# Query, key and weight preparation in the attention projections and the linear attention scan of a two-layer hybrid block

## Chip, core and metric

The kernel runs on one core of one Trainium2 chip. The metric is the device time of one execution in microseconds (us). The engines are named as in the profile: PE is TensorE's matmul (PEld its weight load), DVE is VectorE, ACT is ScalarE, POOL is GpSimd and SP is SyncE, which starts the transfers.

## What is computed

Two layers of one block over 256 context tokens and 1024 latent tokens of width 1024. In each layer one input projection feeds four groups of heads, which are gated, concatenated and projected out:

```python
for l in range(DEPTH):
    hx = rmsnorm(x, norm_g[l]) * (1.0 + sc[:, None]) + sh[:, None]
    px = split_cols(hx @ w_in[l])
    a_l, a_c = diff_attention(px[0:3], ...)
    b_l, b_c = mlstm_mixer(px[3:8], ...)
    c_l, c_c = gla_mixer(px[8:12], ...)
    d_l, d_c = window_gqa(px[12:15], ...)
    y = jnp.concatenate([a_l, b_l, c_l, d_l], axis=-1) * jax.nn.silu(px[15])
    x = x + gt[:, None] * (y @ w_out[l])
```

Three pieces matter here. Both attentions (A: differential, 16 groups of 32 for q and k; D: windowed, 6 groups of 64) normalise q and k and turn them by an angle of the token's place:

```python
q = rmsnorm(q, qn_g)                       # per group of 32 or 64 columns
def _rotate(xh, ang):
    x1, x2 = jnp.split(xh, 2, axis=-1)
    return jnp.concatenate([x1 * cos - x2 * sin, x1 * sin + x2 * cos], axis=-1)
```

The gated linear attention (C, `gla_mixer`) is a scan with a state of 128 x 256 and a decay for each channel:

```python
inter = jnp.einsum('bhtd,bhdv->bhtv', q * jnp.exp(bc), smat)
a = jnp.einsum('bhtd,bhtsd,bhsd->bhts', q, jnp.exp(rel), k)
smat = jnp.exp(b_end)[..., None] * smat + ...
```

## The kernel before

The program is one sequence of stages, each with an instruction list written out by hand for every engine and semaphores between them; an all-engine barrier ends each stage. Nothing is reordered by a scheduler: what stands first in an engine's list runs first. In each of the two layers the order is modulation, norm, B (mLSTM), C (projection, then scan), A, D, gates, output.

**Projections.** `SplitProduct` multiplies in 32-bit parts: every operand is a high part (a rounded copy) and a low part (the rest), and three products are summed. Step i handles one 128-row slice k of one group g of the plan. ACT's `high` copies the tokens' high part (L420, 128x640); DVE's `low` casts the weights' high part and subtracts for their low part (`split_weights`, L383 and L384), then subtracts the tokens' low part (L437); PE's `multiply` (L456) then runs the 15 matmuls of a step. Three buffers (`BUFS` = 3) let ACT and DVE run ahead.

**project_qk** is called for A (L1696; four groups of 8 steps: q and k of tokens 0 to 639, the same of 640 to 1279, then v of each half with weights of 256 columns) and for D (L1903; two groups, v in the same slab). The ten token tiles t of 128 are worked on between the steps, those of a half (`HN` = 5) in the next group's steps: ACT's `keep` squares a tile (L1462), copies it from PSUM to `raw` (L1467) and, for D, v (L1466). DVE's `reduce`, `means`, `refine` and `norm` (L1530 to L1544) make and apply the reciprocal root, in between ACT's `roots` (L1478, L1479, a table load each). POOL multiplies by the gain (L1515) and by the cosine into `rot` (L1520). DVE's `rotate` multiplies by the sine with the two quarters of a pair exchanged, in four instructions (L1555), and adds (L1563 in A; L1569 in D). In D, PE transposes each turned tile (`turns`, L1436: tiles 0 and 1 after step 14, the others after step 15) and ACT keeps it (L1453). `rot` has two slots: POOL's cosine product of tile t waits, for t >= 2, until tile t-2 was turned by DVE (A) or transposed by PE (D). D's second half has no steps beside it: its norm and rotation stand after step 15.

**C's scan** visits 20 tiles, forward and backward in turn. ACT takes the exponentials of a visit (L1241, 8 x 128 columns), POOL scales k (L1229, L1231), DVE scales q (`scale_q`: L1338 a copy of one column, L1339 5 x 128 columns, L1341 128 columns) one visit ahead, PE multiplies (`levels`, `fresh`, `exponents` two visits ahead, `out` one behind), DVE picks the maps out of PSUM (L1370, three per visit) and `finish` updates the state two visits behind (L1347 and L1351 or L1353). `levels` of a visit waits for the three picks of the visit before; `finish` waits for `out`.

## Time and profile before

| | |
|---|---|
| time, median of 3 runs | 2638.15 us (2637.92 to 2640.21) |
| the profiled execution: its time | 2636.37 us |
| its span, first to last instruction | 2634.6 us |
| PE busy | 2109.6 us, 80% |
| DVE busy | 1827.8 us, 69% |
| ACT busy | 1117.2 us, 42% |
| POOL busy | 413.4 us, 16% |
| C's scan, layer 0 and 1 | about 392 to 500 and 1738 to 1850 us |
| A's projection | about 517 to 642 and 1864 to 1989 us |
| D's projection | about 909 to 1009 and 2233 to 2334 us |

Busy shares are averages over stages with different limits, so each stage is read by itself: which engine sits idle, and what ends its idle time. The execution's time has 1.8 us around its span, and lies 1.8 us under the median. The granted clock of PE is a share of its full rate: 1.00 is 2.4 GHz, 0.50 is 1.2 GHz.

### The profile page before, as it was taken

Reading aid. Unit: us, or ns where it says so; the run is one execution under the profiler, and the core shown is the slowest. Engines: PE = TensorE matmul, PEld = TensorE weight load, DVE = VectorE, ACT = ScalarE, POOL = GpSimd, SP = SyncE. Lnnn points to the kernel's source line nnn. Section 1 sums busy time; section 2 is a strip of 40 time slices with the busy share of each in tenths; the row PEclk is TensorE's granted clock in tenths of the full one; section 3 lists DMA queues with packets and bytes.
Section 4 is the critical chain, followed back from the end, with each engine's and each line's share of the span. In section 5 each row is a group of like instructions: output and inputs, shape, how many; then the busy total and the mean of one; then the engine's idle time right before and its main releaser. Section 6 shows DMA issues by size and latency. Waiting matters only on the chain. (4 is left out here: it accounts for less than half of the span.)

```text
span 2634.6 us, 38349 instructions
## 1 busy us (share of the span) xinstructions
PE 2109.6 (80%) x14612; PEld 1765.6 (67%) x14612; DVE 1827.8 (69%) x3505; ACT 1117.2 (42%) x2156; POOL 413.4 (16%) x414
## 2 busy tenths in 40 slices
PE   4968779786888776899987778979767877858988
PEld 2757657666777664788766566767656766647877
DVE  2666668788868667755655576669698796667656
ACT  5433442333757534533215343432435666345321
POOL 0003104222000011022120013025031000110222
PEclk7989887798888887999998898969888988979999
DMA  8100010000000100010424000100000001000121
GB/s 322 79 17 2 17 49 2 2 1 1 1 1 1 49 32 1 21 45 33 158 98 163 19 17 1 49 17 2 1 1 1 1 1 49 32 1 33 37 104 52
DMA packets 18501, 99.48 MB, mean 38 GB/s; under 512 B 2288, under 2 KB 2576, under 8 KB 13072
## 3 DMA queue, kind: packets, MB, share of 16 engines
q1 hardware_dynamic: 12816, 87.51, 8.7%
q10 hardware_dynamic: 5504, 9.52, 1.0%
q8 instruction: 118, 1.93, 0.3%
q14 instruction: 63, 0.52, 0.1%
HBM read 87.50 MB, written 9.44 MB: 37 GB/s over the span
## 5 line engine op out<-in xcount | busy, mean ns | idle before, releaser
L1842 DVE TENSOR_REDUCE a_st<-ps 128x1 f32<-128x1280 f32 (+1 forms) x144 | 196.8, 1369 | 22.9 <-PE ps L1754 22.7
L1813 ACT ACTIVATE ring<-ps,a_st 128x1280 f32<-128x1280 f32 (+1 forms) x144 | 177.3, 1232 | 74.7 <-DVE a_st L1842 74.4
L456 PE MATMUL ps<-a_proj_wh,a_proj_xh 128*128 128x512 f32 (+1 forms) x320 | 118.2, 369 | 63.2 <-DVE a_proj_xl L437 62.4
L2125 PE MATMUL ps<-g_x_hi,g_w_hi 128*128 128x512 f32 (+1 forms) x400 | 148.4, 371 | 10.0 <-DVE g_x_lo L2186 9.5
L2126 PE MATMUL ps<-g_x_lo,g_w_hi 128*128 128x512 f32 (+1 forms) x400 | 147.9, 370 | 0.0
L2127 PE MATMUL ps<-g_x_hi,g_w_lo 128*128 128x512 f32 (+1 forms) x400 | 147.7, 369 | 0.0
L1754 PE MATMUL ps<-a_k,a_q 128*128 128x512 f32 (+1 forms) x400 | 123.8, 419 | 25.8 <-ACT ring L1813 21.3
L2186 DVE TENSOR_TENSOR g_x_lo<-hT,g_x_hi 128x512 fp32r<-128x512 f32 (+1 forms) x120 | 84.4, 708 | 85.6 <-ACT g_x_hi L2149 84.7
L2149 ACT ACTIVATE g_x_hi<-hT 128x512 fp32r<-128x512 f32 (+1 forms) x120 | 70.3, 589 | 158.5 <-PE ps L2127 151.3
L1769 PE MATMUL ps<-cst,ring 128*128 128x128 f32 x656 | 105.5, 294 | 27.4 <-ACT a_aT L1822 16.1
L2260 PE MATMUL ps<-o_w_hi,o_y_hi 128*128 128x512 f32 x288 | 114.5, 398 | 13.1 <-DVE o_y_lo L2291 7.2
L2199 POOL TENSOR_TENSOR yT<-yT,g_gate 128x512 f32<-128x512 f32 (+1 forms) x50 | 61.1, 1229 | 380.9 <-DVE g_gate L2164 235.2
L420 ACT ACTIVATE b_proj_xh<-hT 128x640 fp32r<-128x640 f32 (+1 forms) x64 | 63.9, 1004 | 130.5 <-PE ps L456 104.8
L456 PEld LDWEIGHTS ps<-a_proj_wh,a_proj_xh 128*128 128x128 f32 x320 | 67.5, 211 | 76.2 <-issue 50.8
L456 PE MATMUL ps<-a_proj_wl,a_proj_xh 128*128 128x512 f32 (+1 forms) x320 | 115.1, 360 | 0.0
L456 PE MATMUL ps<-a_proj_wh,a_proj_xl 128*128 128x512 f32 (+1 forms) x320 | 114.5, 358 | 0.0
L2261 PE MATMUL ps<-o_w_lo,o_y_hi 128*128 128x512 f32 x288 | 113.9, 396 | 0.0
L2262 PE MATMUL ps<-o_w_hi,o_y_lo 128*128 128x512 f32 x288 | 113.6, 394 | 0.0
L1769 PEld LDWEIGHTS ps<-cst,ring 128*128 128x128 f32 x656 | 79.6, 150 | 46.7 <-ACT a_aT L1822 23.9
L420 ACT ACTIVATE a_proj_xh<-hT 128x640 fp32r<-128x640 f32 x64 | 46.6, 740 | 149.0 <-PE ps L456 146.8
L2317 ACT ACTIVATE o_y_hi<-yT 128x640 fp32r<-128x640 f32 (+1 forms) x64 | 43.5, 686 | 153.1 <-PE ps L2262 145.6
L1241 ACT ACTIVATE yT<-ps 128x1024 f32<-128x1024 f32 x40 | 41.0, 1024 | 153.5 <-PE ps L1259 153.5
(373 smaller groups left out, 6306.0 us busy)
## 6 DMA issues: line engine op xcount, KB each, us to landing
ring<-in_w SPq DMA_DIRECT2D x22, 2048.0 KB, 7.4
yT<-in_w SPq DMA_DIRECT2D x4, 2048.0 KB, 9.8
latents<-hT ACTq DMA_DIRECT2D x32, 256.0 KB, 2.0
ring<-in_w SPq DMA_DIRECT2D x6, 1024.0 KB, 5.2
hT<-in_tok SPq DMA_DIRECT2D x10, 512.0 KB, 15.1
hT<-in_tok SPq DMA_DIRECT2D x20, 256.0 KB, 5.9
hT<-latents SPq DMA_DIRECT2D x16, 256.0 KB, 5.8
cst<-in_cst SPq DMA_DIRECT2D x1, 2763.0 KB, 14.6
```

The costliest lines, as they stand in the source:

```text
L420: act.activation(self.x_hi[:, i % self.BUFS, 0:m], self.env["hT"][:, k, t0:t0 + m], ACT.Copy).then_inc(self.hi.sem, 1)
L456: last = pe.matmul(out, left, right, start=k == 0 and j == 0, stop=k == KT - 1 and j == 2)
L1754: last = pe.matmul(ps[:, 3 * c + b, 0:w], q4[:, 2 * h + c, t * P:(t + 1) * P], k4[:, 2 * h + c, k0:k0 + w], start=True, stop=True)
L1769: last = pe.transpose(ps[:, 6 + n % 2, (k - a) * P:(k - a + 1) * P], p(u, 0, T)[:, k * P:(k + 1) * P], C(env, "ident"))
L1813: act.activation(p(u, c, n), ps[:, 3 * c:3 * c + 3, :].rearrange("p b n -> p (b n)")[:, 0:n], ACT.Exp, bias=st[:, 0:1], accum_out=st[:, 1: ...
L1842: dve.tensor_reduce(stat[:, u % SLOTS, c, 0:1], ps[:, 3 * c:3 * c + 3, :].rearrange("p b n -> p (b n)")[:, 0:n], AX.X, ALU.max, negate=Tru ...
L2125: pe.matmul(out, w_hi[:, k, cols], x_hi[:, at, 0:b[1]], start=k == 0, stop=False)
L2126: pe.matmul(out, w_hi[:, k, cols], x_lo[:, at, 0:b[1]], start=False, stop=False)
L2127: last = pe.matmul(out, w_lo[:, k, cols], x_hi[:, at, 0:b[1]], start=False, stop=k == KT - 1)
L2260: pe.matmul(ps[:, n % 8, :], y_hi[:, at, tile], w_hi[:, at, :], start=k == 0, stop=False)
L2261: pe.matmul(ps[:, n % 8, :], y_hi[:, at, tile], w_lo[:, at, :], start=False, stop=False)
L2262: last = pe.matmul(ps[:, n % 8, :], y_lo[:, at, tile], w_hi[:, at, :], start=False, stop=k == KT - 1)
```

## The change

1. `SplitProduct` gets `act_weights`, set by `project_qk` alone: ACT makes the weights' high part ahead of the tokens' high part, on a semaphore of its own, and DVE only subtracts. B and C keep the old way.
2. `rotate` makes the sine product in one instruction; the exchange of the two quarters is a step of -1 in its access pattern.
3. In D only, `rot` moves into a free part of `yT` and has five slots (`SLOTS` = `HN`). Tiles 5 to 9 are *late*: ACT copies only their v and leaves q and k in PSUM, DVE's `norm` reads them there, and their cosine product is DVE's and no longer POOL's.
4. In C's scan the three q instructions become one of 6 x 128 columns, into three slots of `qx`; the one-column copy goes to ACT, after the exponentials. `decays`, `qx` and `state` change places in SBUF. `levels` and `out` wait for the same one instruction.

```diff
...
+        if self.act_weights:
+            s, c0, w = self.groups[g][0:3]
+            if k == 0 and (g == 0 or self.groups[g - 1][0] != s):
+                act.wait_ge(self.env["loaded"][s].sem, 16)
+            act.activation(self.w_hi[:, i % self.BUFS, 0:w], slab(self.env, s)[:, k, c0:c0 + w], ACT.Copy).then_inc(self.w_high.sem, 1)
...
+        if self.act_weights:
+            dve.wait_ge(self.w_high.sem, i + 1)
+            dve.tensor_tensor(self.w_lo[:, at, 0:w], slab(self.env, s)[:, k, c0:c0 + w], self.w_hi[:, at, 0:w].bitcast(F32),
+                              ALU.subtract).then_inc(self.weights.sem, 1)
...
+                    end = P - 1 if UNITS[u][0] == 0 else 0
+                    act.wait_ge(decay_ready.sem, u + 1)
+                    if u >= 4:
+                        act.wait_ge(finished.sem, u - 3)
+                    act.activation(start[:, u % 4:u % 4 + 1], decays[u % 2][:, 7, end:end + 1], ACT.Copy).then_inc(start_kept.sem, 1)
...
-                    dve.tensor_copy(start[:, u % 4:u % 4 + 1], d[:, 7, end:end + 1])
-                    dve.tensor_tensor(qx[:, u % 2, :, :], d[:, 2:7, :], qT[:, span(u)].unsqueeze(1).broadcast_to([P, 5, P]), ALU.mult)\
+                    dve.tensor_tensor(qx[:, u % 3, :, :], decays[u % 2][:, 2:8, :], qT[:, span(u)].unsqueeze(1).broadcast_to([P, 6, P]), ALU.mult)\
                        .then_inc(q_scaled.sem, 1)
-                    dve.tensor_tensor(from_start[:, u % 3, :], d[:, 7, :], qT[:, span(u)], ALU.mult).then_inc(q_scaled.sem, 1)
...
+        def late(t):
+
+            return not halves and t >= HN
...
+                if late(t):
+                    act.activation(v_dst(t), bank[:, v0:v0 + nv], ACT.Copy).then_inc(v_kept.sem, 1)
+                    return
...
-                if t >= 2:
+                if late(t):
+                    continue
+                if t >= SLOTS:
 
-                    pool.wait_ge(rotated.sem if halves else turned.sem, t - 1)
+                    pool.wait_ge(rotated.sem if halves else turned.sem, t - SLOTS + 1)
...
-                for i in range(2):
-                    for f in range(2):
-                        ins = dve.tensor_tensor(y[:, :, f, i, :], x[:, :, f, 1 - i, :],
-                                                s[:, f, i, :].unsqueeze(1).broadcast_to([P, groups, q4]), ALU.mult)
-                        dv.mark(ins)
+                dv.mark(dve.tensor_tensor(y, x[:, :, :, ::-1, :], s.unsqueeze(1).broadcast_to([P, groups, 2, 2, q4]), ALU.mult))
+                if late(t):
+                    if t >= SLOTS:
+                        dve.wait_ge(turned.sem, t - SLOTS + 1)
+                    dv.mark(dve.tensor_tensor(grouped(rot[:, t % SLOTS, :]), grouped(raw[:, t % HN, :]),
+                                              cos[:, t, :].unsqueeze(1).broadcast_to([P, groups, width]), ALU.mult))
+                else:
+                    dve.wait_ge(cos_ready.sem, t + 1)
...
```

On DVE, one steady visit of the scan, from the state's update to the picks; before:

```order
L1347 SCALAR_TENSOR_TENSOR ring<-ring,c_start,ps 128x256
L1353 COPY yT<-ps 128x256
L1338 COPY c_start<-yT 128x1
L1339 TENSOR_TENSOR c_qx<-yT,c_qT 128x640
L1341 TENSOR_TENSOR c_from_start<-yT,c_qT 128x128
L1370 COPY_PREDICATED ring<-cst,ps 128x512 x3
```

and after (the visit shown is one that adds to an earlier result, so its second row is a sum and no copy):

```order
L1358 SCALAR_TENSOR_TENSOR c_state<-c_state,c_start,ps 128x256
L1362 TENSOR_TENSOR yT<-ps,yT 128x256
L1350 TENSOR_TENSOR yT<-c_decays,c_qT 128x768
L1381 COPY_PREDICATED ring<-cst,ps 128x512 x3
```

Three rows between `finish` and the picks became one.

On DVE, D's projection, from the rotation of tiles 2 and 3 to that of tile 4, with step 15's parts between; before:

```order
L1555 TENSOR_TENSOR ring<-d_raw,cst 128x6x16 x4
L1569 TENSOR_TENSOR ring<-ring 128x384
L1555 TENSOR_TENSOR ring<-d_raw,cst 128x6x16 x4
L1569 TENSOR_TENSOR ring<-ring 128x384
L383 CAST d_proj_wh<-ring 128x512
L384 TENSOR_TENSOR d_proj_wl<-ring,d_proj_wh 128x512
L437 TENSOR_TENSOR d_proj_xl<-hT,d_proj_xh 128x640
L1555 TENSOR_TENSOR ring<-d_raw,cst 128x6x16 x4
L1569 TENSOR_TENSOR ring<-ring 128x384
```

and after:

```order
L1579 TENSOR_TENSOR ring<-d_raw,cst 128x384
L1597 TENSOR_TENSOR yT<-yT,ring 128x384
L1579 TENSOR_TENSOR ring<-d_raw,cst 128x384
L1597 TENSOR_TENSOR yT<-yT,ring 128x384
L439 TENSOR_TENSOR d_proj_wl<-ring,d_proj_wh 128x512
L448 TENSOR_TENSOR d_proj_xl<-hT,d_proj_xh 128x640
L1579 TENSOR_TENSOR ring<-d_raw,cst 128x384
L1597 TENSOR_TENSOR yT<-yT,ring 128x384
```

The cast left the list, four sine rows became one, and the order of the rest stands.

On POOL, the last gain and cosine of D's first half and its second half, after the change (before, the two kinds alternate for all ten tiles):

```order
L1535 TENSOR_TENSOR d_raw<-d_raw,par 128x384
L1542 TENSOR_TENSOR yT<-d_raw,cst 128x384
L1535 TENSOR_TENSOR d_raw<-d_raw,par 128x384
L1542 TENSOR_TENSOR yT<-d_raw,cst 128x384
L1535 TENSOR_TENSOR d_raw<-d_raw,par 128x384 x5
```

The second half has gains alone on POOL.

## Rows read from the trace of the kernel before

**Rows 1.** D's projection by layer; busy us (x instructions), PE's clock, DMA share, GB/s.
```profile
909.00:1009.00 100.00, 67.20 (x270) 52.83 (x270) 66.19 (x128) 31.96 (x64) 21.53 (x20) 0.79 0.06 22
...
2233.00:2334.00 101.00, 67.48 (x270) 52.92 (x270) 66.20 (x129) 31.97 (x64) 21.93 (x22) 0.79 0.06 21
```

**Rows 2.** The page's groups: busy us, mean ns | idle before, what ended it.
```profile
L456 PE MATMUL ps<-a_proj_wh,a_proj_xh 128*128 128x512 f32 (+1 forms) x320 | 118.2, 369 | 63.2 <-DVE a_proj_xl L437 62.4
```

**Rows 3.** Timeline of D's projection, DVE: start, us, what, [idle before <-releaser].
```profile
951.58 1.24 DVE L384 TENSOR_TENSOR d_proj_wl<-ring,d_proj_wh 128x512 fp32r<-128x512 f32 x1
952.74 1.63 DVE L437 TENSOR_TENSOR d_proj_xl<-hT,d_proj_xh 128x640 fp32r<-128x640 f32 x1
...
968.87 1.26 DVE L1569 TENSOR_TENSOR ring<-ring 128x384 f32<-128x384 f32 x1 [4.58 <-POOL ring L1520]
...
982.92 0.56 DVE L1569 TENSOR_TENSOR ring<-ring 128x384 f32<-128x384 f32 x1 [7.35 <-POOL ring L1520]
...
991.02 4.70 DVE L1544 TENSOR_TENSOR d_raw<-d_raw,d_stat 128x384 f32<-128x384 f32 x5
...
1006.83 0.56 DVE L1569 TENSOR_TENSOR ring<-ring 128x384 f32<-128x384 f32 x1
```

**Rows 4.** The same timeline on POOL and, last, on ACT.
```profile
951.34 0.93 POOL L1520 TENSOR_TENSOR ring<-d_raw,cst 128x384 f32<-128x384 f32 x1
952.23 1.47 POOL L1515 TENSOR_TENSOR d_raw<-d_raw,par 128x384 f32<-128x384 f32 x1
...
985.85 0.55 ACT L1462 ACTIVATE ring<-ps 128x384 f32<-128x384 f32 x1
```

**Rows 5.** The same timeline on PE.
```profile
963.76 0.47 PE L456 MATMUL ps<-d_proj_wh,d_proj_xh 128*128 128x512 f32 x1 [0.86 <-DVE d_proj_xl L437]
...
975.04 0.77 PE L456 MATMUL ps<-d_proj_wh,d_proj_xh 128*128 128x512 f32 x1 [6.97 <-DVE d_proj_xl L437]
```

**Rows 6.** Tiles of A and D: duration ns min/median/max, first and last start.
```profile
L383 DVE CAST a_proj_wh<-ring x64: 279/416/1532, 517.7 to 1984.7; 128x512 fp32r<-128x512 f32 x32, 128x256 fp32r<-128x256 f32 x32
...
L1555 DVE TENSOR_TENSOR ring<-a_raw,cst x80: 277/284/1374, 569.1 to 1983.7; 128x128 f32<-128x128 f32 x80
...
L1544 DVE TENSOR_TENSOR a_raw<-a_raw,a_stat x20: 678/691/1781, 557.5 to 1953.2; 128x512 f32<-128x512 f32 x20
...
L1544 DVE TENSOR_TENSOR d_raw<-d_raw,d_stat x20: 545/886/1375, 949.4 to 2318.7; 128x384 f32<-128x384 f32 x20
L1515 POOL TENSOR_TENSOR d_raw<-d_raw,par x20: 985/1123/1467, 950.0 to 2326.9; 128x384 f32<-128x384 f32 x20
L1520 POOL TENSOR_TENSOR ring<-d_raw,cst x20: 864/1058/1328, 951.3 to 2329.4; 128x384 f32<-128x384 f32 x20
```

**Rows 7.** ACT's groups by form: busy us, mean ns, idle before.
```profile
L420 ACT ACTIVATE c_proj_xh<-hT 128x512 fp32r<-128x512 f32 x16 | 10.2, 636 | 8.1 <-PE ps L456 8.1
```

**Rows 8.** A steady visit of C's scan on DVE, timeline.
```profile
442.79 0.48 DVE L1347 SCALAR_TENSOR_TENSOR ring<-ring,c_start,ps 128x256 f32<-128x256 f32 x1
...
443.85 0.15 DVE L1338 COPY c_start<-yT 128x1 f32<-128x1 f32 x1 [0.24 <-DVE yT L1353]
...
445.16 2.25 DVE L1370 COPY_PREDICATED ring<-cst,ps 128x512 f32<-128x512 uint32 x3
```

**Rows 9.** The same visit on POOL and PE, with PE's next start.
```profile
442.56 1.54 POOL L1229 TENSOR_TENSOR c_kx<-yT,c_kT 128x640 f32<-128x640 f32 x1 [2.08 <-ACT yT L1241]
...
442.95 0.95 PE L1272 MATMUL ps<-c_qx,c_kx 32*128 32x128 f32 x24 [0.26 <-DVE ring L1370]
...
446.15 1.00 PE L1309 MATMUL ps<-yT,ring 128*128 128x64 f32 x8
...
447.56 0.95 PE L1272 MATMUL ps<-c_qx,c_kx 32*128 32x128 f32 x24 [0.41 <-DVE ring L1370]
```

**Rows 10.** The scan's q instructions, both layers: ns min/median/max.
```profile
L1339 DVE TENSOR_TENSOR c_qx<-yT,c_qT x40: 814/842/2200, 394.4 to 1837.4; 128x640 f32<-128x640 f32 x40
...
L1341 DVE TENSOR_TENSOR c_from_start<-yT,c_qT x40: 283/541/550, 396.6 to 1838.2; 128x128 f32<-128x128 f32 x40
```

More of the change, by code:

```diff
@@ L387, with __init__ @@
 class SplitProduct:
-    def __init__(self, nc, env, own, name, groups, bufs=2):
-        self.env, self.groups, self.BUFS = env, groups, bufs
+    def __init__(self, nc, env, own, name, groups, bufs=2, act_weights=False):
+        self.env, self.groups, self.BUFS, self.act_weights = env, groups, bufs, act_weights
         self.steps = [(g, k) for g in range(len(groups)) for k in range(KT)]
@@ L1304, in out @@
                         pe.wait_ge(finished.sem, u - 1)
-                    pe.wait_ge(q_scaled.sem, 2 * (u + 1))
-                    pe.matmul(out_bank(u), from_start[:, u % 3, :], state[:, way, :], start=True, stop=False, skip_group_check=True)
+                    pe.wait_ge(q_scaled.sem, u + 1)
+                    pe.matmul(out_bank(u), qx[:, u % 3, 5, :], state[:, way, :], start=True, stop=False, skip_group_check=True)
                     pe.wait_ge(picked.sem, 3 * (u + 1))
@@ L1384, in project_qk @@
     nch = n_qk // P
-    sq_ready, reduced, ms_ready, root, normed, gained, cos_ready, rotated, dv, turned, kept = (
+    sq_ready, reduced, ms_ready, root, normed, gained, cos_ready, rotated, dv, turned, kept, v_kept = (
         signal(f"{name}_{n}") for n in ("square", "reduced", "mean", "root", "normed", "gained", "cos", "rotated",
-                                        "dve", "turned", "turned_kept"))
+                                        "dve", "turned", "turned_kept", "v_kept"))
     s_v, v0, nv, v_dst = v_of
@@ L1406, in project_qk @@
         else:
-            rot = spare[:, 3 * n_qk:5 * n_qk].rearrange("p (u c) -> p u c", u=2)
+            rot = env["yT"][:, 6:8, :].rearrange("p a t -> p (a t)")[:, 0:HN * n_qk].rearrange("p (u c) -> p u c", u=HN)
+        SLOTS = 2 if halves else HN
         stat = tile("stat", [P, 3, HN * groups])
         ms, rstd, tmp = (stat[:, i, :] for i in range(3))
-        proj = SplitProduct(nc, env, own, f"{name}_proj", plan, 3)
+        proj = SplitProduct(nc, env, own, f"{name}_proj", plan, 3, act_weights=True)
         cos = C(env, f"cos_{name}").rearrange("p (t w) -> p t w", t=NT)
@@ L1435, in turns @@
                 for c in range(nch):
-                    last = pe.transpose(ps[:, 6 + t % 2, c * P:(c + 1) * P], rot[:, t % 2, c * P:(c + 1) * P], C(env, "ident"))
+                    last = pe.transpose(ps[:, 6 + t % 2, c * P:(c + 1) * P], rot[:, t % SLOTS, c * P:(c + 1) * P], C(env, "ident"))
                 last.then_inc(turned.sem, 1)
@@ L1500, in _ @@
                 roots(1)
+                act.wait_ge(v_kept.sem, HN)
             else:
@@ L1507, in _ @@
                 act.wait_ge(kept.sem, NT)
-            act.wait_ge(proj.read.sem, proj.first[-1])
+            act.wait_ge(proj.read.sem, proj.first[-1] if halves else HN)
         @block.gpsimd
@@ L1541, in norm @@
             def norm(t):
-                dve.wait_ge(proj.read.sem, t + 1)
+                if not late(t):
+                    dve.wait_ge(proj.read.sem, t + 1)
                 x = grouped(raw[:, t % HN, :])
-                dve.tensor_tensor(x, x, of_tile(rstd, t).unsqueeze(2).broadcast_to([P, groups, width]), ALU.mult)\
+                if late(t):
+                    dve.wait_ge(v_kept.sem, t - HN + 1)
+                    dve.wait_ge(rotated.sem, t - HN + 1)
+                dve.tensor_tensor(x, grouped(ps[:, t % BANKS, 0:n_qk]) if late(t) else x, of_tile(rstd, t).unsqueeze(2).broadcast_to([P, groups, width]), ALU.mult)\
                    .then_inc(normed.sem, 1)
@@ L1568, in rotate @@
                 else:
-                    dve.tensor_tensor(rot[:, t % 2, :], rot[:, t % 2, :], turn[:, :], ALU.add).then_inc(rotated.sem, 1)
+                    dve.tensor_tensor(rot[:, t % SLOTS, :], rot[:, t % SLOTS, :], turn[:, :], ALU.add).then_inc(rotated.sem, 1)
             def half_step(h, k):
```

41 lines of the change are left out of this document (20 added, 21 removed).

## The prediction

> **What bounds the kernel now.** I read the groups of the page first, then the three stages the change touches, each by its stretch, its waits and its timelines.
>
> D's projection has DVE busy for 66.19 of 100 us and PE for 67.20, PE at a mean granted clock of 0.79; layer 1 repeats it within 0.3 us [rows 1]. So no engine bounds it throughout, and the waits tell. DVE's last sum of tile 2 stands still for 4.58 us and that of tile 4 for 7.35 us, each time for POOL's cosine product [rows 3], which has only two slots and waits until PE has transposed the tile two before. PE does that only after step 14 and after step 15, and step 15 itself is held up by DVE, which hangs in the first of these waits: PE sits idle for 6.97 us before it and starts again at the lower clock (0.77 us for its first matmul, against 0.47 us after a gap of 0.86) [rows 5]. It is a ring of waits and no lack of speed.
>
> In A's projection PE sits idle for 62.4 us over both layers because DVE's low part is late [rows 2]. There DVE is the bound, and POOL stretches it: where both work, each instruction of the one waits for the end of one of the other. DVE's subtraction at 951.58 should need some 0.69 us, as any product of 512 columns [rows 6], and ends with 1.24; it starts under POOL's 951.34 and goes on when that ends, at 952.27. POOL's next ends at 953.70, and the 640-column subtraction of 952.74 ends at 954.37, 0.67 us later [rows 3, 4]. In such stretches DVE's and POOL's times add up.
>
> In C's scan two chains are level. DVE's own goes from `finish` at 442.79 by q's first instruction at 443.85 and the picks at 445.16 to the next `finish` after 2.15 us: 1.06 + 1.31 + 2.15 = 4.52 us a visit [rows 8]. The other runs over two visits: PE from `levels` at 442.95 to the end of `out` at 447.15 is 4.20 us, 0.10 to `finish`, then 1.06 + 1.31 to the picks, and 2.40 from their start (445.16) to the next `levels` at 447.56: 9.07 us, or 4.53 a visit [rows 8, 9].
>
> **The change part by part.** The sum is made against the profiled execution; its 2636.37 us lie 1.8 under the median, which I add back by subtracting the sum from the median.
>
> *D, first half.* DVE loses a cast of 0.42 and 0.04 of gap in each step, 0.46 us. A sine product becomes one of 384 columns; its nearest row is the norm's 0.545 [rows 6], against four instructions that take 0.76 together, so about 0.2 less. Against that, ACT's high part of the weights (128x512) costs 0.64 us, some 0.5 from start to start [rows 7]. While PE needs 3.4 us a step this is free; in steps 9 to 11 it stands before ACT's squares and roots, and delays the first norm from 949.36 by about 0.7. Then POOL, no longer held, runs all ten products of the half at a stretch: 5 x (0.985 + 0.864) = 9.2 us [rows 6], about 4.5 of them now beside DVE's work for steps 13 and 14. Walking the alternation of rows 3 and 4 through the new order (0.88 and 0.74 for POOL's two kinds when it follows on DVE; 0.40, 0.55 and 0.67 for DVE's norm and its two subtractions) gives DVE's last subtraction of step 13 at 960.4, of 14 at 966.0, of 15 at 969.7. Steps 13 and 14 start later than now (966.1 against 963.76 for the latter), but step 15 follows the two transposes at 970.5 against 975.04. With gaps of about 2 us instead of 7 I take PE's clock to stay at its upper level, 0.68 us a sum: all five sums are ready at 973.9, and tile 9 is squared at 974.05 against 985.85 [rows 4].
>
> *D, second half.* From that square to the first norm at 991.02 there are 5.17 us, of which ACT's copy to `raw` (0.37 to the next start) goes: norms start at 978.85. That is 12.2 us less. Before, five norms took 4.70 us, stretched by POOL [rows 3]. Now one operand lies in PSUM. The scan's update with a PSUM operand takes 0.48 us while POOL works [rows 8, 9], so I take these norms as not stretched, 0.48 apart, 2.4 together. POOL's five gains (1.0 each) go on beside them. DVE has 15 products of 384 columns, 1.62 a tile with the two gaps; three gains still stretch the first two tiles. Step by step the last sum ends 13.2 us after the first norm's start, against 16.4 now (991.02 to 1007.39 [rows 3]); the added cosine products eat most of what POOL gives. The last sum comes at 992.05 instead of 1007.39: 15.3 us a layer, **30.6 for both**. Unknown are the clock in step 15 (at the lower level, 1.28 us a sum, 2.7 us less gain), the norms (stretched as now, 2.3 less) and the alternation (one POOL product more or less on the path of each of steps 13 to 15, up to 2 either way): 10 to 18 a layer.
>
> *A.* `rot` keeps two slots here. On DVE's path lie 4 casts of 512 columns (0.46 each) and 9 of 256 (0.28 and a gap, 0.32) [rows 6], 4.7 us; and ten sine products. Four instructions of 128 columns at 0.284 take 0.89 together, one of 512 takes 0.69 [rows 6] and 0.04 goes with the gaps: 0.25 each, 2.5 us. Back come 0.7 and 0.6 by ACT's later roots in the two halves, 0.6 where ACT makes high parts after the v copies at step 26, and 0.9 since one more POOL product falls between the norms once the cast no longer meets it. 7.2 - 2.8 = 4.4 us a layer, **8.8 for both**. Bounds: 2 (the stretches follow POOL's work alone) and 7.2 (nothing comes back).
>
> *C's scan.* A 768-column product costs 0.814 + 128 x (0.814 - 0.283)/512 = 0.95 us [rows 10]; to the next start 0.86, so the 1.31 between `finish` and picks becomes 0.86. DVE's chain falls to 4.07, the two-visit one to 8.62, 4.31 a visit; PE's own 4.20 lies just below. POOL's product of k comes nearer to DVE's, since both follow on PE: up to 0.14 on the q product, 4.38. I take 0.19 us a visit for the 14 visits per layer that run in this way, and 0.5 a layer for the first visits, where the q product is stretched to 2.2 us [rows 10]: 3.2 a layer, **6.3 for both**. While PE runs at 1.2 GHz, `finish` waits for it and nothing is gained. Bounds 1 and 9. ACT's one-column copy and its wait lie under 3.6 us of ACT's idle time in each visit; without that cover it would cost 0.2 a visit. `start` is needed a visit or more later.
>
> A rule of the Trainium skill speaks against moving the casts: ScalarE: Activation LUTs, Rules for kernel authors, wants simple elementwise work on VectorE, as ScalarE is slower for each element. The trace agrees on the price, 636 ns on ACT [rows 7] against 416 on DVE [rows 6]. By that rule the move would be a loss of about 0.2 us a step on whichever engine is the bound; that engine is DVE here, ACT being idle for some two thirds of these stages, so it changes the gain only where ACT stands on the path, and that is counted above.
>
> Sum: 30.6 + 8.8 + 6.3 = 45.7 us. 2638.15 - 45.7 = **2592.5 us**.
>
> **The rivals.** (1) *POOL set free costs more.* With no wait left, POOL's cosine products of tiles 2 to 4 meet DVE's low parts for steps 13 and 14, PE's gaps there grow to 3 us or more, and its clock falls for step 15. For it: DVE's and POOL's times add up today wherever both work [rows 3, 4]. Against it: POOL's work is only 9.2 us. 2.7 for the clock and 2 to 4 for the gaps a layer: 2602 to 2607, say 2604. (2) *Only D gains.* In A, DVE's time goes into waiting for POOL all the same, and in the scan PE takes over at its present pace: 2638.15 - 30.6 = 2607.5. Against it: A's steps 27 to 31 lose casts with POOL mostly idle. (3) *More than I see.* A's PE gaps shorten enough to keep its upper clock and the stretches shrink with DVE's count of instructions, 7 us a layer in A, 17 in D: 2638 - 14 - 34 - 8 = 2582. (4) *The change doesn't do what it says*: the waits for the transposes come back as DVE's wait for a free slot. Tile 5 needs the transpose of tile 0, done after step 14; this would bring at most some 7 us a stage back only if PE's transposes of tiles 2 to 4 were late, which needs ACT's copies; 2638. (5) *Slower.* The sine product reads its operand with a step of -1 between runs of 8 or 16 columns. No row shows such a pattern. If it ran slower for each element, all 40 such products (10 a stage, four stages) would carry it, nearly all on DVE's path. It turns the sign when it eats the 45.7 us and 5.3 beyond: 51/40 = 1.3 us each, 1.9 instead of 0.6. The row against it: runs of 8 columns with gaps already cost nothing, 284 ns [rows 6] against 283 for a whole row of 128 [rows 10]; only the sign of the step is new. At such a price: 2645.
>
> **How the numbers follow.** Forecast 0.55 (2584 to 2600 by the middle of its bounds), rival 1 0.20, rival 2 0.06, rival 3 0.13, rival 4 0.03, rival 5 0.03. The range 2580 to 2609 holds the forecast, rivals 1 and 2 and half or more of 3. A measurement of this kernel tells 0.2%, 5.3 us, from no change. Faster than that: the first four, 0.94; within it: rival 4, 0.03; slower: 0.03.
>
> **What would show it.** D's 4.58 and 7.35 us waits of DVE for POOL gone, PE's gap before step 15 under 1 us, both D stages near 85 us; PE's clock 1.00 in step 15 (0.50 speaks for rival 1). The late norms near 0.55 us each with POOL busy. Sine products 0.69 and 0.55 us where POOL is idle (much more is rival 5). A's stages about 4 us shorter, PE's waits for DVE's low part near 45 us instead of 62.4. The scan's visits 4.3 to 4.4 us apart. I am wrong in the size above all if the alternation in steps 12 to 15 goes otherwise, since D is two thirds of the sum.

## The result

The changed kernel takes 2600.3 us (median of 4, 2598.0 to 2612.7) against 2639.2 us (4, 2637.9 to 2640.7) before: a ratio of 0.986, 95% interval 0.983 to 0.990. It is 38.8 us faster; the prediction was 45.7, and its 2592.5 us (0.982 of the time before) lies just under the interval, within the range given. A second series of the same kernel gave 2588.2 us (2583.3 to 2596.5) against 2642.2, a ratio of 0.980 (0.978 to 0.982), 54 us faster. The forecast lies between the two, and what stands between them is the larger lesson of this case.

Two traces can be laid side by side stage by stage, since PE makes the same 14612 matmuls in both. A stage lasts here from PE's first matmul of it to that of the next (D, A: the projections of the two attentions; scan: C's scan; B: the mLSTM stage with its projection; rest: all else). The table gives us of the profiled executions, read off these two traces:

```
                     before          changed         difference       forecast
D, layer 0 / 1        98.6 / 98.8    83.9 / 83.1    -14.6 / -15.7    -15.3 each
A, layer 0 / 1       142.4 / 143.1  138.3 / 138.9    -4.1 / -4.2      -4.4 each
scan, layer 0 / 1    128.7 / 126.7  129.1 / 112.0    +0.4 / -14.8     -3.2 each
attention A, 0 / 1   249.3 / 226.5  251.1 / 233.3    +1.8 / +6.8       0
B, layer 0 / 1       234.5 / 231.7  235.3 / 233.6    +0.8 / +1.9       0
rest                  954.1          957.5            +3.4             0
span                 2634.6         2596.2           -38.4           -45.7
```

D and A do what was worked out, D within 0.3 us of the sum. The scan is far off in both directions, and stages that nothing touches lost 14.7 us.

**D.** First its two layers in the windows view of the changed kernel (us; busy us of PE, PEld, DVE, ACT, POOL with instructions; PE's clock, DMA share, GB/s), against [rows 1]:

```profile
912.00:995.91 83.91, 64.83 (x270) 51.18 (x270) 55.80 (x86) 36.07 (x72) 18.74 (x17) 0.87 0.07 25
2211.47:2294.59 83.12, 65.35 (x270) 51.62 (x271) 55.78 (x86) 36.07 (x72) 18.72 (x17) 0.85 0.07 26
```

Then layer 0's timeline on DVE, on POOL and on PE (start, us, what, idle before and releaser):

```profile
958.67 1.61 DVE L448 TENSOR_TENSOR d_proj_xl<-hT,d_proj_xh 128x640 fp32r<-128x640 f32 x1
...
963.96 0.56 DVE L1597 TENSOR_TENSOR yT<-yT,ring 128x384 f32<-128x384 f32 x1
...
980.14 2.42 DVE L1570 TENSOR_TENSOR d_raw<-ps,d_stat 128x384 f32<-128x384 f32 x5
...
992.74 0.56 DVE L1597 TENSOR_TENSOR yT<-yT,ring 128x384 f32<-128x384 f32 x1
```

```profile
980.77 5.87 POOL L1535 TENSOR_TENSOR d_raw<-d_raw,par 128x384 f32<-128x384 f32 x5 [17.33 <-DVE d_raw L1570]
```

```profile
960.43 0.47 PE L467 MATMUL ps<-d_proj_wh,d_proj_xh 128*128 128x512 f32 x1 [2.47 <-DVE d_proj_xl L448]
966.00 0.47 PE L467 MATMUL ps<-d_proj_wh,d_proj_xh 128*128 128x512 f32 x1 [1.93 <-DVE d_proj_xl L448]
...
967.10 0.63 PE L467 MATMUL ps<-d_proj_wh,d_proj_xh 128*128 128x512 f32 x1
...
968.38 0.63 PE L467 MATMUL ps<-d_proj_wh,d_proj_xh 128*128 128x512 f32 x1
...
971.68 0.48 PE L467 MATMUL ps<-d_proj_wh,d_proj_xh 128*128 128x512 f32 x1
```

The sums of tiles 2 and 4 have no wait for POOL in front of them, where [rows 3] had 4.58 and 7.35 us. PE waits 2.47 and 1.93 us before steps 13 and 14 and not at all before step 15 (971.68, right behind its own transposes; in layer 1 the waits are 2.47, 0.79 and none), where [rows 5] had 6.97. The five late norms take 2.42 us together beside POOL's gains; in [rows 3] they took 4.70.

**A.** The page's group that answers to [rows 2]:

```profile
L467 PE MATMUL ps<-a_proj_wh,a_proj_xh 128*128 128x512 f32 (+1 forms) x320 | 117.9, 368 | 55.4 <-DVE a_proj_xl L448 54.3 <-ACT a_proj_xh L426 1.1
```

PE waits 54.3 us for DVE's low part instead of 62.4: 8.1 us less, which is the gain of both A stages (8.3).

**The scan.** A steady visit of the changed kernel on DVE, against [rows 8]:

```profile
465.12 0.48 DVE L1358 SCALAR_TENSOR_TENSOR c_state<-c_state,c_start,ps 128x256 f32<-128x256 f32 x1 [0.35 <-ACT c_start L1257]
465.52 0.42 DVE L1364 COPY yT<-ps 128x256 f32<-128x256 f32 x1
466.18 1.02 DVE L1350 TENSOR_TENSOR yT<-ring,c_qT 128x768 f32<-128x768 f32 x1 [0.24 <-DVE yT L1364]
467.13 2.25 DVE L1381 COPY_PREDICATED ring<-cst,ps 128x512 f32<-128x512 uint32 x3
469.29 0.46 DVE L1358 SCALAR_TENSOR_TENSOR c_state<-c_state,c_start,ps 128x256 f32<-128x256 f32 x1
```

The visits are 4.17 and 4.57 us in turn, 4.37 on average, where they were 4.54. The joined product takes 0.95 us to the start of the picks. But the whole stage shows something else. The windows of the scan, before, changed layer 0, changed layer 1:

```profile
390.99:519.71 128.72, 105.81 (x1460) 89.50 (x1461) 98.30 (x188) 34.48 (x57) 50.45 (x42) 0.78 0.01 2
```

```profile
393.43:522.54 129.11, 109.10 (x1460) 92.21 (x1461) 89.33 (x147) 38.88 (x79) 51.40 (x42) 0.74 0.01 2
1727.31:1839.26 111.95, 90.54 (x1456) 76.97 (x1457) 87.90 (x143) 37.10 (x73) 54.93 (x42) 0.91 0.01 2
```

DVE's busy time fell by 9 us in both layers (98.30 to 89.33, 96.82 to 87.90), as the joined product should make it. PE's clock was 0.74 in the one and 0.91 in the other, and that decided. In layer 0 three distances between two `finish` are 7.2 to 7.3 us long, since DVE waits for PE at the lower clock:

```profile
412.49 0.48 DVE L1358 SCALAR_TENSOR_TENSOR c_state<-c_state,c_start,ps 128x256 f32<-128x256 f32 x1 [2.82 <-PE ps L1324]
...
419.83 0.48 DVE L1358 SCALAR_TENSOR_TENSOR c_state<-c_state,c_start,ps 128x256 f32<-128x256 f32 x1 [2.83 <-PE ps L1324]
```

In layer 1 there is none, the time to the first `finish` is 15.8 instead of 19.1 us, and the last two distances are 3.95 and 1.40 instead of 5.88 and 2.56.

**The untouched stages.** The attention of layer 1, before and changed: the same 1249 matmuls, the same busy time on DVE, ACT and POOL, and another clock.

```profile
2008.92:2235.45 226.53, 178.05 (x1249) 155.63 (x1249) 180.87 (x257) 154.21 (x276) 6.58 (x10) 0.91 0.04 15
```

```profile
1978.13:2211.47 233.34, 185.47 (x1249) 162.64 (x1249) 180.72 (x256) 154.54 (x278) 6.58 (x10) 0.87 0.04 14
```

Most of the difference arises in 20 us of it. Three windows at about the same place of the program, before, then changed; the last of each block is the first half of those 20 us:

```profile
2075.00:2085.00 10.00, 9.20 (x72) 8.39 (x71) 9.35 (x12) 7.96 (x15) 0.00 (x0) 1.00 0.01 2
2085.00:2095.00 10.00, 7.77 (x62) 6.80 (x62) 6.98 (x11) 5.97 (x12) 0.00 (x0) 1.00 0.00 0
2095.00:2105.00 10.00, 8.09 (x66) 7.22 (x65) 1.15 (x4) 1.51 (x3) 0.00 (x0) 0.95 0.01 2
```

```profile
2045.00:2055.00 10.00, 9.19 (x73) 8.39 (x71) 9.37 (x13) 7.96 (x15) 0.00 (x0) 1.00 0.01 2
2055.00:2065.00 10.00, 7.77 (x63) 6.81 (x61) 6.90 (x11) 5.88 (x12) 0.00 (x0) 1.00 0.00 0
2065.00:2075.00 10.00, 9.40 (x46) 8.61 (x44) 0.57 (x2) 1.50 (x3) 0.00 (x0) 0.52 0.00 0
```

PE was as busy in the 20 us ahead (9.20 and 9.19, 7.77 and 7.77), and then worked at the upper of its two levels (2.4 GHz) in the one trace and at the lower (1.2 GHz) in the other: 66 matmuls against 46 in 10 us.

### The profile page after: what moved, and what is told of

The parts are those of the page before. It is cut to its first block and busy times, and to the rows that moved or that the text cites. A ratio compares the mean times of both kernels' runs of the same rounds, so it can differ in the third digit from the quotient of the medians.

```text
span 2596.2 us, 38279 instructions
## 1 busy us (share of the span) xinstructions
PE 2106.9 (81%) x14612; PEld 1766.7 (68%) x14612; DVE 1767.3 (68%) x3219; ACT 1163.9 (45%) x2282; POOL 418.6 (16%) x404
## 3 DMA queue, kind: packets, MB, share of 16 engines
q8 instruction: 118, 1.93, 0.3%
## 5 line engine op out<-in xcount | busy, mean ns | idle before, releaser
L467 PE MATMUL ps<-a_proj_wh,a_proj_xh 128*128 128x512 f32 (+1 forms) x320 | 117.9, 368 | 55.4 <-DVE a_proj_xl L448 54.3
L467 PE MATMUL ps<-b_proj_xh,b_proj_wh 128*128 128x512 f32 (+1 forms) x192 | 72.9, 380 | 41.1 <-ACT yT L629 26.4
L1890 DVE SCALAR_TENSOR_TENSOR ring<-ring,a_st 128x1280 f32<-128x1280 f32 (+1 forms) x72 | 102.6, 1425 | 0.1
```

Source lines behind the costliest of these rows:

```text
L467: last = pe.matmul(out, left, right, start=k == 0 and j == 0, stop=k == KT - 1 and j == 2)
L1890: dve.scalar_tensor_tensor(out=p(u, 0, n), in0=p(u, 1, n), scalar=st[:, 0, 3:4], in1=p(u, 0, n), op0=ALU.mult, op1=ALU.add).then_inc(comb. ...
```

## Experiments

The theory after the first look: the change is worth what was worked out (D 30, A 8, the scan its shorter visits, some 4.5), and the clock of stages it doesn't touch takes some of it back or adds to it. The rival: the new timing of the stages costs a fixed price elsewhere, or the parts are worth something else. In each case below the ratio is to the kernel before, run beside it (medians 2642.2, 2639.3, 2639.7 and 2639.7 us in the four series).

**after_again.** No edit.

> The changed kernel once more, for its scatter. In its first trace the stages that the change does not touch took 13.7 us more than before, at a lower granted clock (two stretches in the differential attention, 5.8 to 6.7 us each, and some in the mLSTM stage), and the scan of the second layer 15 us less, of which some 10 are the clock too. Theory 1 (accidents of the clock, different from run to run): this trace has its stretches at the lower level at other places of the untouched stages, the times scatter over 2598 to 2613 us, median 2600 to 2605. Theory 2 (the new timing of the stages brings them): the same stretches again, times within 0.2% of 2600.

2588.2 us (2583.3 to 2596.5), ratio 0.980 (0.978 to 0.982). The scan of layer 0 now takes 116.7 us instead of 129.1, with the same code:

```profile
392.20:508.91 116.71, 95.66 (x1460) 80.39 (x1461) 90.25 (x147) 38.89 (x79) 52.15 (x42) 0.87 0.01 2
```

All its visits are short. That is 12.4 of the 14.7 us between the two traces; 1.4 come from the first 69 us of the program. The attentions repeat to 0.1 us (251.2 and 233.35). So neither theory holds alone, and both had the median too high: what the clock does in the attentions repeats in this kernel's two traces, and what it does in the first visits of the scan varies from run to run. Over the two series the times of this kernel span 29 us; those of the kernel before span 5.8 us in 36 timed runs of all series (2637.9 to 2643.7).

**after_old_scan.** The scan as before, the projections as changed: the scan's part of the change reversed, among it

```diff
-                    dve.tensor_tensor(qx[:, u % 3, :, :], decays[u % 2][:, 2:8, :], qT[:, span(u)].unsqueeze(1).broadcast_to([P, 6, P]), ALU.mult)\
+                    dve.tensor_copy(start[:, u % 4:u % 4 + 1], d[:, 7, end:end + 1])
+                    dve.tensor_tensor(qx[:, u % 2, :, :], d[:, 2:7, :], qT[:, span(u)].unsqueeze(1).broadcast_to([P, 5, P]), ALU.mult)\
                        .then_inc(q_scaled.sem, 1)
+                    dve.tensor_tensor(from_start[:, u % 3, :], d[:, 7, :], qT[:, span(u)], ALU.mult).then_inc(q_scaled.sem, 1)
```

> The changed kernel with the old linear attention scan (five-block query product and a sixth of its own, start value kept by DVE). The trace of the changed kernel has a visit at 4.37 us where the old one has 4.53, at full clock. Theory 1 (the scan's part of the change is worth its visits, about 28 x 0.16 = 4.5 us, and the rest is the clock): 2604 to 2608 us, visits 4.53. Rival (PE and not DVE holds the scan, so the joined product gives nothing that lasts): 2599 to 2602.

2605.3 us (2602.8 to 2615.3), ratio 0.987 (0.985 to 0.990), within theory 1's band. That is no proof of it: the band was set by the first series' 2600, and beside this version the changed kernel took 2588.2, 17 us less, where the visits explain some 4.5. Of the 20.4 us between the two traces 18.9 stand in the two scans, most of them the clock. Its visits are 4.54 us. Layer 0 begins with visits of 7.35 us, with PE at its lower level (128.7 us for the stage), layer 1 has none of these (118.9 us), so an early rise of the clock isn't a thing of the new scan alone.

**d_alone.** D's part only:

```diff
-        proj = SplitProduct(nc, env, own, f"{name}_proj", plan, 3, act_weights=True)
+        proj = SplitProduct(nc, env, own, f"{name}_proj", plan, 3, act_weights=not halves)
...
+                if halves:
+                    for i in range(2):
+                        for f in range(2):
+                            dv.mark(dve.tensor_tensor(y[:, :, f, i, :], x[:, :, f, 1 - i, :],
+                                                      s[:, f, i, :].unsqueeze(1).broadcast_to([P, groups, q4]), ALU.mult))
+                else:
```

and the old scan.

> Only the D projection as in the changed kernel (five slots, late norms from the bank, late cosine products on DVE, ScalarE's high part of the weights, one sine product); A projection and scan as before. Theory 1 (D gives 14.0 and 15.3 us in the two layers by the traces): 2639.2 - 29.3 = 2610 us. Rival (part of this difference is clock that A's and the scan's parts bring or take): below 2605 or above 2614.

2609.4 us (2606.1 to 2611.7), ratio 0.988 (0.986 to 0.989); 2610 was expected. D's stages are 82.8 and 83.9 us. PE's wait for the low part in A is back at 62.7 us. But the total hides a balance: in its trace the scan of layer 1 won 10 us by the clock, and the attentions changed by -4.6 and +7.8.

This trace also tells what the scan's part is worth apart from the visits at the lower level. Its layer 1 has none of them, as the changed kernel's layer 1, with the old code:

```profile
1722.65:1839.29 116.64, 92.61 (x1456) 78.56 (x1457) 95.72 (x184) 32.70 (x51) 51.07 (x42) 0.90 0.01 2
```

116.6 against 112.0: 4.7 us less with the new code. Of that 2.7 are the 17 distances between `finish` of steady visits, at 0.16, and 1.9 the way to the first `finish` (17.76 against 15.84). But on that way the clock isn't equal. The way in d_alone, then in the changed kernel:

```profile
1722.65:1740.41 17.76, 14.01 (x150) 11.15 (x154) 11.68 (x17) 4.10 (x4) 10.26 (x9) 0.71 0.00 1
1727.31:1743.15 15.84, 12.45 (x152) 9.77 (x156) 9.59 (x12) 4.91 (x8) 9.77 (x9) 0.78 0.01 2
```

PE worked 14.01 us in the one and 12.45 in the other on the same part of the program, at 0.71 and at 0.78, and those 1.6 us are most of the 1.9. Where PE stood at 0.50 all the way, the old code took 19.34 us to the first `finish` and the new 19.06, 0.3 less. So at an equal clock the scan's part is worth about 2.7 + 0.3 = 3.0 us a layer when all visits run at the upper level, and 4.7 is its upper bound.

**before_delayed.** The kernel before, and a pure delay ahead of A's first step:

```diff
                 dv.link(dve, dve.tensor_scalar(gain, gain, width ** -0.5, None, ALU.mult))
+                for _ in range(12):
+                    dv.link(dve, dve.memset(turn[:, :], 0.0))
```

> The kernel before, with a pure delay and no other edit: DVE writes zeros 12 times to a scratch row ahead of the first step of the A projection, in both layers, some 4 to 6 us each. Question: do stages that nothing touches change their time when they only start later? In the traces the differential attention of the second layer takes 226.5 us in the kernel before and 233.3 to 234.8 us in four kernels that start it at another time (one of them with its own A stage unchanged). Theory 1 (the granted clock follows the point in time at which the stage starts, not the change): attention stages or scans change by 2 to 12 us, in either direction, and the whole is not before plus the delays. Rival (it follows the work itself): every other stage within 1 us of before, the whole longer by 8 to 12 us.

2655.1 us (2651.6 to 2655.8), ratio 1.0055 (1.004 to 1.007). The delays are 8.0 us each, 16 in all; the whole grew by 15.8 by the medians and by 19.4 in the traces. Inside, the attention of layer 0 became 5.4 us shorter and that of layer 1 7.9 us longer, with no edit in either:

```profile
2018.76:2253.22 234.46, 185.99 (x1249) 163.06 (x1249) 180.94 (x257) 154.31 (x276) 6.56 (x10) 0.87 0.04 14
669.57:913.48 243.91, 195.39 (x1316) 169.94 (x1317) 195.07 (x309) 166.94 (x322) 6.57 (x10) 0.90 0.04 14
```

This is theory 1: a stage whose own work is the same can be 2% shorter or 3.5% longer. The 7.9 us are about what the changed kernel lost there (6.8). The A stage of layer 0, old code in both traces, was 2.7 us shorter too (139.7). What time of start or what history brings which pattern isn't known from these runs: the changed kernel started this stage at 1978 and at 1963 us, with 233.3 both times; two variants below had 229.6 and one 227.1.

**d_two_slots.** As changed, but POOL's cosine product waits for the transpose two tiles back:

```diff
-                if t >= SLOTS:
+                if t >= 2:
 
-                    pool.wait_ge(rotated.sem if halves else turned.sem, t - SLOTS + 1)
+                    pool.wait_ge(rotated.sem if halves else turned.sem, t - 1)
```

> The changed kernel, but in D's first half POOL's cosine product of tile t waits for the transpose of tile t-2 again, as with two slots; late norms and late products on DVE stay. D's projection takes 83.9 and 83.1 us in the changed kernel. Theory 1 (the ring of waits, POOL for PE's transpose and DVE for POOL, was the larger part): DVE waits for POOL again at tiles 2 and 4, PE has a gap of 5 us or more before step 15, D's projection 91 to 96 us. Rival (ScalarE's weight parts and the joined sine product gave most, and the slots little): 84 to 87 us.

2603.6 us (2600.2 to 2605.1), ratio 0.986. D's stages are 92.8 and 91.3 us, 8.5 a layer more, and the ring of waits is back in the old form, on DVE and on PE:

```profile
954.35 1.33 DVE L1597 TENSOR_TENSOR yT<-yT,ring 128x384 f32<-128x384 f32 x1 [4.74 <-POOL yT L1542]
...
967.17 0.56 DVE L1597 TENSOR_TENSOR yT<-yT,ring 128x384 f32<-128x384 f32 x1 [7.04 <-POOL yT L1542]
```

```profile
959.80 0.77 PE L467 MATMUL ps<-d_proj_wh,d_proj_xh 128*128 128x512 f32 x1 [6.18 <-DVE d_proj_xl L448]
```

So the three added slots are over half of D's 15 us.

**d_no_late.** As changed, D's second half like its first:

```diff
-            return not halves and t >= HN
+            return False
...
```

> The changed kernel, but D's second half runs as its first: ScalarE copies each tile to its row before DVE's norm reads it, POOL makes gain and cosine product of all ten tiles. By the working of the prediction this gives back 0.4 us before the first late norm, 2.3 us of stretched norms and 0.9 us of rotation: 3 to 5 us a layer, D's projection 86 to 88.5 us, whole 2 x 4 above the changed kernel. Rival (DVE pays with the added cosine products what POOL saves): D's projection 83 to 84.5 us.

2596.1 us (2588.0 to 2602.4), ratio 0.984. D's stages are 87.0 and 86.3 us, 3.2 more a layer, as expected. The norms are the stretched ones again:

```profile
965.64 4.70 DVE L1569 TENSOR_TENSOR d_raw<-d_raw,d_stat 128x384 f32<-128x384 f32 x5
```

0.94 us apart with both operands in SBUF, 0.48 with one in PSUM, each time beside POOL's gains. The Trainium skill (SBUF — State Buffer, Who interferes with whom) says that a DVE instruction with two inputs in SBUF contends with a GpSimd one that reads SBUF, and that one with at most one input there, outside the 2-port modes, doesn't; this pair of traces agrees.

**four_sines.** As changed, the sine product in four instructions again, in A and D:

```diff
-                dv.mark(dve.tensor_tensor(y, x[:, :, :, ::-1, :], s.unsqueeze(1).broadcast_to([P, groups, 2, 2, q4]), ALU.mult))
+                for i in range(2):
+                    for f in range(2):
+                        dv.mark(dve.tensor_tensor(y[:, :, f, i, :], x[:, :, f, 1 - i, :],
+                                                  s[:, f, i, :].unsqueeze(1).broadcast_to([P, groups, q4]), ALU.mult))
```

> The changed kernel with the sine product in four instructions again, in both projections; all else as changed. A's stage takes 138.3 and 138.9 us in the changed kernel (first projection matmul to the first score matmul), D's 83.9 and 83.1. Theory (the prediction's terms: 0.25 us for each of A's ten products, all on DVE's path; 0.2 for D's, of which the five late ones and two or three early ones lie on the path): A's stage 140.5 to 141.5 us, D's 84.5 to 85.5. Rival (the joined product's 0.69 and 0.55 us hide behind POOL's): A's stage within 1 us of the changed kernel's.

2594.5 us (2590.1 to 2597.8), ratio 0.983 (0.981 to 0.984). A's stages 139.7 and 140.3 us, D's 85.2 and 85.7: 1.4 more in A and 1.9 in D, on average of the layers. The expectation had 2 to 3 in A; there the term was too large by some 1 us a layer. PE's wait in A is 58.3 us, 4.0 more. The stage times alone wouldn't show it in A: in the nine traces with A and its order as changed, A's stages lie between 137.4 and 140.0 us. The waits do (51.2 to 55.9 in those nine), and so do D's stages, which lie between 82.8 and 84.1 in the eight traces with D as changed.

**dve_weights.** As changed, the weights' high part made by DVE:

```diff
-        proj = SplitProduct(nc, env, own, f"{name}_proj", plan, 3, act_weights=True)
+        proj = SplitProduct(nc, env, own, f"{name}_proj", plan, 3, act_weights=False)
```

> The changed kernel with the weights' high part made by DVE again in both projections, all else as changed. Theory (the prediction's terms: in A the casts on the path are worth 4.7 us, and 2.8 come back by ScalarE's later roots and POOL): A's stage 139.7 to 141 us, against 138.3 and 138.9; in D steps 12 to 15 lose 0.46 each and the roots come 0.7 earlier, so D's projection 84.5 to 86 us, against 83.9 and 83.1. Rival (ScalarE's later roots and squares cost what DVE saves): both stages within 0.7 us of the changed kernel's, and the weights' move is worth nothing.

2588.5 us (2583.2 to 2602.8), ratio 0.981 (0.979 to 0.983). A's stages 139.3 and 138.9 us, D's 84.3 and 84.2: 0.5 more in A, 0.7 in D. A comes nearer to the rival (0.95 and 0.04), D lies between the two (0.3 and 1.1). Yet PE's waits in A are 58.1 us, 3.8 more over both layers, and 58.3 + 58.1 - 54.3 gives 62.1, next to the 62.4 of the kernel before (with the scatter of 51.2 to 55.9 so close a match is in part luck). The waits add up and the stage times don't, since in that trace A ran at a higher clock in layer 0 (a mean clock of 0.92, against 0.89 in the changed kernel). Of this part the case shows by the waits that it gains, and that the gain is small, not how small.

**start_on_dve.** As changed, the start value kept by DVE:

```diff
-                    act.activation(start[:, u % 4:u % 4 + 1], decays[u % 2][:, 7, end:end + 1], ACT.Copy).then_inc(start_kept.sem, 1)
...
+                    dve.tensor_copy(start[:, u % 4:u % 4 + 1], decays[u % 2][:, 7, end:end + 1]).then_inc(start_kept.sem, 1)
```

> The changed kernel with the scan's one-column copy of the start value on DVE again, ahead of its query product. A visit takes 4.37 us at full clock in the changed kernel. Theory (it stands in both chains of DVE, and DVE's is not covered): 4.45 to 4.6 us a visit, 2 to 6 us in all. Rival (the profile names ScalarE's copy as what finish waits for, 0.3 us every second visit; on DVE that wait goes): 4.2 to 4.35 us.

2588.5 us (2582.5 to 2590.5), ratio 0.980 (0.978 to 0.981), and 4.37 us a visit: neither theory. Three rows of its DVE timeline tell why:

```profile
462.46 0.48 DVE L1355 SCALAR_TENSOR_TENSOR c_state<-c_state,c_start,ps 128x256 f32<-128x256 f32 x1 [0.24 <-PE ps L1319]
...
463.52 0.15 DVE L1346 COPY c_start<-ring 128x1 f32<-128x1 f32 x1 [0.24 <-DVE yT L1359]
463.59 0.96 DVE L1347 TENSOR_TENSOR yT<-ring,c_qT 128x768 f32<-128x768 f32 x1
464.47 2.25 DVE L1378 COPY_PREDICATED ring<-cst,ps 128x512 f32<-128x512 uint32 x3
```

The copy costs 0.07 us from start to start, and the product behind it 0.88 instead of 0.95. And `finish` still waits before every second visit (0.22 to 0.24 us, where the changed kernel has 0.32 to 0.35), now with PE's output product named. The name "ACT c_start" in the changed kernel was the last of several releases in time and not the cause: PE's output product ended there within 0.02 us of it.

**out_first and out_first_deep.** If PE's output product is what holds `finish`, it should stand ahead of the exponents:

```diff
                     fresh(u)
-                    if u + 2 < NU:
-                        exponents(u + 2)
                     if u >= 1:
                         out(u - 1)
+                    if u + 2 < NU:
+                        exponents(u + 2)
```

> The changed kernel, with PE's output product of visit u-1 ahead of the exponents of visit u+2 instead of behind them. In the trace of the changed kernel DVE's finish waits for the end of that output product (0.33 us before every second finish), and the exponents' six matmuls stand 1.15 us ahead of it. Theory 1 (the chain over two visits, 8.73 us, is the bound now; DVE's own is 4.1 a visit): visits at 4.1 to 4.2 us at full clock, 28 x 0.2 = 6 us less, 2594 us; nothing gained in the visits at the lower clock. Rival (ScalarE's late copy of the start value is what finish waits for, as the profile names it): the exponents come later, so does the copy, and the visits stay at 4.37 or grow.

2583.3 us (2583.2 to 2588.4), ratio 0.978 (0.977 to 0.980), beside the 2588.2 of the changed kernel. The visits are 4.20 and 4.44 in turn, 4.32, outside the 4.1 to 4.2 of the theory: a quarter of the gain hoped for. The median is 4.9 us lower, yet layer 0's scan is 1.2 us longer than in after_again (117.9), so the whole doesn't measure the edit. DVE's query product waits for the decays now:

```profile
1777.81 0.96 DVE L1350 TENSOR_TENSOR yT<-ring,c_qT 128x768 f32<-128x768 f32 x1 [0.59 <-ACT ring L1251]
```

So the exponents were made a visit earlier too (`exponents(u + 3)` in the loop, `exponents(2)` ahead of it):

> The changed kernel with PE's output product ahead of the exponents, and the exponents made one visit earlier (of visit u+3 instead of u+2). With the output product first the visits went to 4.32 us, not 4.15: DVE's query product waited 0.36 and 0.59 us for ScalarE's exponential, which waited for the exponents' end. Theory 1: with the exponents a visit ahead that wait goes, DVE's own chain (1.06 + 0.95 + 2.15 = 4.16 us) and PE's work bound the scan: 4.2 us a visit at full clock, 28 x 0.17 = 4.8 us less than the changed kernel at an equal clock. Rival (POOL's key product, starting earlier, stretches DVE's picks and finish): 4.3 us or more.

> The kernel out_first_deep once more, with more rounds, since its times scatter (2570 to 2594 us). Its trace shows visits of 4.19 us where the changed kernel has 4.37: 28 x 0.18 = 5 us less, at an equal clock. Theory: median 2577 to 2590 us, a ratio to the kernel before of 0.976 to 0.980, below the changed kernel's 0.980 to 0.986; visits 4.19 again at full clock. Rival (the gain lies inside the scatter of the clock and the first median was luck): median 2588 or above.

The visits are 4.19 us with hardly an exception, in both series. 2577.5 us (2570.5 to 2594.5), ratio 0.977 (0.974 to 0.981), then 2578.3 us (2564.3 to 2589.7), ratio 0.9745 (0.972 to 0.977). The second interval lies below both of the changed kernel's, the first overlaps the lower one. It is the fastest version of this case: 61 to 62 us under the kernel before, some 10 under the changed one's 2588. By the visits, 5 of these are explained; the rest isn't.

## Why the prediction was right, and where it was off

*D, first half: right.* The walk through the alternation held: DVE's low parts for steps 13, 14 and 15 ended at 960.28, 965.86 and 969.88 (forecast 960.4, 966.0, 969.7), though the stage began 0.55 us later. Step 15 came at 971.7 instead of 970.5: in step 14 PE ran at its lower level for some 3 us (1.28 us from one sum to the next at 967.10, where 0.69 is usual), which the forecast had not in it; step 15 itself ran at the upper level, as taken. Tile 9 was squared at 975.41 instead of 974.05, 1.4 us late. Layer 0 fell 0.7 us short of the 15.3, layer 1 came out 0.4 above. In layer 1 it was the first half of step 13 that ran at the lower level (2260.36 to 2263.4), with 0.79 us of waiting still behind it.

*D, second half: right.* Norms from 980.14, 2.42 us together (forecast 2.4), last sum's end 13.2 us after the first norm, as worked out. d_no_late puts this half at 3.2 us, d_two_slots the slots at 8.5; with 1.9 for the sine product and 0.7 for the weights, each undone by itself, that makes 14.3 of the 15.2 us.

*Rival 1* (POOL set free costs more) is refuted by the PE rows above: gaps of 2.47 and 1.93 us, not 3 or more, and no wait ahead of step 15. The fall of the clock that it named did come, but in step 14 (in layer 1 in step 13), for about half of it and not for a whole step. *Rival 4* is refuted by the waits that are gone, and *rival 3* by stages that gave 15 and 4 us and not 17 and 7.

*A: the sum right, its parts not separately shown.* 4.1 and 4.2 us against 4.4. The sine product was put at 2.5 a layer and gave 1.4 of stage time and 2.0 of PE's waits when undone; the weights' part (4.7 less 2.8, 1.9) gave 0 to 1 of stage time and 1.9 of waits. The text's own check, PE's waits "near 45 us", was a slip: 62.4 less the 8.8 of the sum makes 53.6, and 54.3 was measured. *Rival 2* (only D gains) falls with that, and with the scan's 4.37 us a visit against 4.54.

*Rival 5* (a step of -1 is slow) is refuted by the sine products' own times, 676 ns at the least and 689 in the median in A, and in D:

```profile
L1579 DVE TENSOR_TENSOR ring<-d_raw,cst x20: 552/560/1218, 960.2 to 2290.3; 128x384 f32<-128x384 f32 x20
```

as a product of 384 columns takes in plain order.

*The scan: mechanism right, the clock missing.* 4.31 to 4.38 us a visit was worked out, and 4.37 measured; 0.19 was taken for each and 0.16 came, since the joined product needs 0.95 us to the next start and not 0.86. At an equal clock the scan gives about 3.0 us a layer instead of 3.2 (4.7 at most): 17 visits gain and not 14, as none runs at the lower level, and the first visits give 0.3 instead of 0.5. Visits at the lower clock gain nothing, as it said (7.35 and 7.27 us before, 7.34, 7.33 and 7.18 after). The covered copy on ACT is covered; but "would cost 0.2 a visit" on DVE is refuted, it would cost nothing.

*What was missing* is a term for the clock in the scan and in the untouched stages. The sum added up the edits and let everything else stand as in one trace. With the scan at an equal clock the parts make about 30.3 + 8.3 + 6.0 = 44.6 us (48 with the scan at its upper bound), close to the sum. In the first trace the other stages took back 14.7 and the scans gave another 8.4 by the clock (14.4 less 6.0); in the second trace the scans gave 26.8 in all. Measured medians: 38.8 and 54.0. That 2592.5 lies between them is luck and no merit of the method: a range of 2580 to 2609 was wide enough for this scatter because of other doubts. The Trainium skill (TensorE: Matmul & The Clock Gate, What's actually happening) says that the clock's monitor runs freely and that the same kernel can therefore start with different numbers of slow matmuls from run to run. The two traces of the same kernel differ in that way in the middle of the program too; their 12.4 us in one scan are 0.5% of the span.

## What to carry to other kernels

A ring of waits between three engines (DVE for POOL, POOL for PE's transpose, PE for DVE's next operand) doesn't show as anyone's high load; more slots in its buffer gave 8.5 us a stage where a joined instruction gave 1 to 2. When an edit's gain is compared by traces, compare stage by stage, and take the untouched stages as the measure of how far the clock alone moves time: here by up to 8 us in an attention stage and 12 in a scan of one and the same kernel, in either direction. A band for the whole time that was set beside one series proves little beside another. When the profile names a wait's releaser, see whether another of the awaited instructions ended at the same moment, before moving work away from the one that is named.

## What the runs showed of the hardware

- Pure delays of 8 us, one in each layer, changed an untouched stage of 226.5 us by +7.9 and another of 249.3 by -5.4, through PE's granted clock (0.91 to 0.87, and 0.87 to 0.90), with the busy time of DVE, ACT and POOL the same to 0.1 us. What selects the pattern stays open.
- The first visits of the scan have two forms, one with PE at the lower level (7.3 us a visit) and one at the upper (4.2 to 4.6), 8 to 15 us a stage apart for the same layer and the same code. In all 28 scans on record PE's granted clock falls to the lower level 6.6 to 7.3 us before the scan's first matmul; how long it stays there differs. With the old code (four traces, two layers) it was 41.0 us in six scans and 13.7 in two. With the new code in PE's old order (seven traces) it was 47.8 us in four scans, 23.9 in seven and 13.7 in three. Only 41.0 and 47.8 bring visits of 7.3 us. Neither what ends the stretch nor whether the shorter visit brings the other lengths is shown; if it does, that would explain why the kernel before scatters so little.
- A DVE product of 384 fp32 columns with one operand in PSUM took 548 ns, with both in SBUF 545 at the least. Beside GpSimd's gains the first is not stretched (559 at most), and the second is (1218 in the median in d_no_late).
- A one-column DVE copy shows 0.15 us in the trace and costs 0.07 from start to start ahead of a long product.
